# Delta layer of a fused model: the exponentials of the decay in three parts, masks behind the low splits, VectorE's work between the levels of the inverse, and extra multiplications of constants around the turning of x

## What is computed

```python
proj = x @ w_in                                    # 1024 -> 4096 + 16
qkv = silu(causal_depthwise_conv(proj[:, :3072], conv_w))
q = l2_normalize(qkv[:, :1024]) * 128 ** -0.5; k = l2_normalize(...); v = ...
g = -exp(a_log) * softplus(a + dt_bias);  beta = sigmoid(bt)
gc = cumsum(g);  decay = exp(where(causal, gc_i - gc_j, -inf))
a_strict = where(i > j, (k * beta) @ k.T * decay, 0)
u = triangular_solve(a_strict + eye, v * beta)
w = triangular_solve(a_strict + eye, k * beta * exp(gc))
qk = (q @ k.T) * decay
# then, from chunk to chunk: v_new = u - w @ state; o = (q * exp(gc)) @ state + qk @ v_new
y = (rms_norm(o, norm_w) * silu(z)) @ w_o
```

## Time and profile before

| | before |
|---|---|
| median of 3 executions | 2284.34 us |
| their lowest and highest | 2279.2, 2288.88 us |
| the profiled execution | 2281.05 us |
| its span, first to last instruction | 2279.3 us |
| mean granted TensorE clock | 0.986 |
| PE / DVE / ACT / POOL busy | 2181.7 / 1649.5 / 1202.6 / 149.0 us |

### The profile page before, as it was taken

One profiled execution on the slowest core, in us unless ns is written; L12 is line 12 of the kernel. 1 busy time (PEld: TensorE's weight loads), 2 busy tenths in 40 slices (PEclk: granted clock), 3 DMA queues, 4 the chain that ended last, 5 costly groups with the idle time before them and its releaser, 6 DMA issues.

```text
span 2279.3 us, 40684 instructions
## 1 busy us (share of the span) xinstructions
PE 2181.7 (96%) x16637; PEld 2032.2 (89%) x16637; DVE 1649.5 (72%) x2278; ACT 1202.6 (53%) x1717; POOL 149.0 (7%) x175
## 2 busy tenths in 40 slices
PE   7879999999889999999999999999999999999998
PEld 7878978879678887999988899999999988899998
DVE  6674588854858887777865757777877776758776
ACT  5755567763747776433456545333533456545433
POOL 2022000000000000000410001000000220001000
PEclk9999999999999999999999999999999999999999
DMA  8420379959135995555643345555555563346552
GB/s 220 159 93 21 115 272 336 342 181 208 38 96 227 332 328 205 167 172 183 173 144 100 105 137 178 178 181 181 173 174 166 161 179 98 121 152 204 167 200 77
DMA packets 257021, 395.53 MB, mean 174 GB/s; under 512 B 16937, under 2 KB 204194, under 8 KB 256866
## 3 DMA queue, kind: packets, MB, share of 16 engines
q1 hardware_dynamic: 251874, 380.15, 49.8%
q0 software_dynamic: 4880, 13.13, 3.2%
q10 hardware_dynamic: 112, 0.05, 0.0%
HBM read 385.43 MB, written 7.86 MB: 173 GB/s over the span
## 4 chain that ended last, share of the span: by engine, by line
PE 49%; DVE 5%; ACT 3%; DMA 2%; issue 1%; ACTq 0%; DVEq 0%; SPq 0%
PE psum_banks L345 15%; PE psum_banks L347 14%; PE psum_banks L346 14%; DVE weights_low L754 2%; DMA weight_ring<-w_in 2%; PE psum_banks L3300 1%; ACT weights_high L1960 1%; PE psum_banks L3306 1%; PE psum_banks L3325 1%; ACT weights_high L748 1%; DVE source_low L617 1%; PE psum_banks L3335 0%; PE psum_banks L3366 0%; DVE rstd L637 0%; DVE h L780 0%
## 5 line engine op out<-in xcount | busy, mean ns | idle before, releaser
L345 PE MATMUL psum_banks<-source_high,weights_high 128*128 128x272 f32 (+1 forms) x2656 | 780.5, 294 | 21.0 <-DVE weights_low L1967 9.2
L347 PE MATMUL psum_banks<-source_high,weights_low 128*128 128x272 f32 (+1 forms) x2656 | 765.3, 288 | 0.0
L346 PE MATMUL psum_banks<-source_low,weights_high 128*128 128x272 f32 (+1 forms) x2656 | 764.5, 288 | 0.0
L345 PEld LDWEIGHTS psum_banks<-source_high,weights_high 128*128 128x128 f32 x2656 | 508.2, 191 | 29.0 <-DVE weights_low L1967 10.8
L346 PEld LDWEIGHTS psum_banks<-source_low,weights_high 128*128 128x128 f32 x2656 | 508.6, 192 | 1.0
L347 PEld LDWEIGHTS psum_banks<-source_high,weights_low 128*128 128x128 f32 x2656 | 507.5, 191 | 0.0
L1967 DVE TENSOR_TENSOR weights_low<-weight_ring,weights_high 128x2048 fp32r<-128x2048 f32 x102 | 236.2, 2315 | 181.8 <-ACT weights_high L1960 181.3
L748 ACT ACTIVATE weights_high<-weight_ring 128x2048 fp32r<-128x2048 f32 x131 | 242.4, 1910 | 182.7 <-PE psum_banks L347 181.5
L754 DVE TENSOR_TENSOR weights_low<-weight_ring,weights_high 128x2048 fp32r<-128x2048 f32 x131 | 293.1, 2289 | 62.4 <-ACT weights_high L748 62.2
L1960 ACT ACTIVATE weights_high<-weight_ring 128x2048 fp32r<-128x2048 f32 x102 | 194.6, 1908 | 63.2 <-PE psum_banks L347 46.3
L345 PE MATMUL psum_banks<-hidden_high,weights_high 128*128 128x272 f32 (+1 forms) x704 | 203.5, 289 | 1.1 <-DVE h L780 1.0
(11 more groups left out here) (516 smaller groups left out, 3834.2 us busy)
## 6 DMA issues: line engine op xcount, KB each, us to landing
weight_ring<-ffn_w_in SPq DMA_DIRECT2D x88, 1024.0 KB, 6.7
weight_ring<-w_in SPq DMA_DIRECT2D x48, 1024.0 KB, 5.2
weight_ring<-ffn_w_out SPq DMA_DIRECT2D x44, 1024.0 KB, 4.9
weight_ring<-moe_w_down SPq DMA_DIRECT2D x24, 1024.0 KB, 6.8
weight_ring<-moe_w_gate SPq DMA_DIRECT2D x44, 512.0 KB, 4.9
weight_ring<-moe_w_up SPq DMA_DIRECT2D x44, 512.0 KB, 6.5
weight_ring<-gdn_w_in SPq DMA_DIRECT2D x16, 1024.0 KB, 6.4
more_ring<-moe_w_gate SPq DMA_DIRECT2D x32, 512.0 KB, 4.9
```

The source lines that it names most:

```text
L345: pe.matmul(out, w_hi, x_hi, start=start, stop=False)
L346: pe.matmul(out, w_hi, x_lo, start=False, stop=False)
L347: return pe.matmul(out, w_lo, x_hi, start=False, stop=stop)
```

## The change

1. **PE, start.** Ten multiplications of `full_ones` by itself (128x128, f32) stand ahead of `turn_x`, fourteen between it and tile 0. Nobody reads them. The wait for the constant moves ahead of them.
2. **PE, square sums.** Behind tile 12 none, then 7; 8 and 9; 10 and 11; 12; none behind 17; from 18 on as before.
3. **ScalarE.** `decay` is in three parts at t = 9, 10, 11: first the exponentials of the row and the two small ones, which wait for `rows` only; then that of QK, which waits for both masks; then that of A. `silu(7)` to `silu(12)` move to t = 12, 13, 14, two at each.
4. **VectorE, masks.** From t = 5 and 6 to t = 6 and 8, so that each stands behind a `lin.low` and a `conv`.
5. **VectorE, inverse.** q times the decays moves behind level 0, `lin.low` of panel 16 behind level 1, `fall` behind level 3.

```diff
--- before.py
+++ after.py
@@ -2196,8 +2196,13 @@
                         mm = turn(3 + 2 * t, lambda h: v[:, h, chunk[t]])
                     mm.then_inc(pe_n.sem, 1)
 
+                summed_behind = {12: [], 13: [7], 14: [8, 9], 15: [10, 11], 16: [12], 17: []}
+                pe.wait_ge(pr.ones_set.sem, pr.ones_set.at(2))
+                for _ in range(10):
+                    pe.matmul(ps[:, 2, 0:P], pr.full_ones, pr.full_ones, start=True, stop=True)
                 turn_x()
-                pe.wait_ge(pr.ones_set.sem, pr.ones_set.at(2))
+                for _ in range(14):
+                    pe.matmul(ps[:, 2, 0:P], pr.full_ones, pr.full_ones, start=True, stop=True)
                 for t in range(GDN_OUT):
                     lin.multiply(pe, t, source.hi, source.lo, arrive if t == 0 else None)
                     if t == 0:
@@ -2206,8 +2211,9 @@
                         turn_params()
                     if t == 3:
                         decay_rows()
-                    if 0 <= t - 5 < GDN_V:
-                        square_sum(t - 5)
+                    for n in summed_behind.get(t, [t - 5]):
+                        if 0 <= n < GDN_V:
+                            square_sum(n)
                     if t >= GDN_OUT - 6:
                         prepare(t - (GDN_OUT - 6))
                 for n in range(6, 9):
@@ -2321,13 +2327,17 @@
                     do(act.activation(soft, neg_abs, ACT.Exp))
                     act.activation(soft, soft, ACT.Ln, bias=1.0).then_inc(act_n.sem, 1)
 
-                def decay():
-                    act.wait_ge(dve_n.sem, dve_n.at(D_MASK))
-                    act.activation(flat4(QK), flat4(QK), ACT.Exp)
-                    act.activation(flat4(A), flat4(A), ACT.Exp)
-                    act.activation(flat(exp_row[:, :, :]), flat(bank2(6)), ACT.Exp)
-                    act.activation(exp_gc, gc, ACT.Exp)
-                    act.activation(to_last, to_last, ACT.Exp).then_inc(act_n.sem, 1)
+                def decay(part):
+                    if part == 0:
+                        act.wait_ge(dve_n.sem, dve_n.at(D_ROWS))
+                        act.activation(flat(exp_row[:, :, :]), flat(bank2(6)), ACT.Exp)
+                        act.activation(exp_gc, gc, ACT.Exp)
+                        act.activation(to_last, to_last, ACT.Exp)
+                    elif part == 1:
+                        act.wait_ge(dve_n.sem, dve_n.at(D_MASK))
+                        act.activation(flat4(QK), flat4(QK), ACT.Exp)
+                    else:
+                        act.activation(flat4(A), flat4(A), ACT.Exp).then_inc(act_n.sem, 1)
 
                 def sums_out(p):
                     act.wait_ge(ss_mm.sem, ss_mm.at(2 * p + 2))
@@ -2367,9 +2377,12 @@
                         act.wait_ge(pe_n.sem, pe_n.at(P_AB))
                         act.activation(ab[:, :, :], ps[:, 3, 0:32].rearrange("p (t c) -> p t c", t=2), ACT.Copy).then_inc(act_n.sem, 1)
                         small()
-                    if t == 9:
-                        decay()
-                    if 2 <= t < 22:
+                    if t in (9, 10, 11):
+                        decay(t - 9)
+                    elif t in (12, 13, 14):
+                        silu(2 * t - 17)
+                        silu(2 * t - 16)
+                    elif 2 <= t < 22:
                         silu(t - 2)
                     if t >= 7 and t % 2 and t <= 21:
                         sums_out((t - 7) // 2)
@@ -2547,8 +2560,8 @@
                         steps()
                     if t == 4:
                         rows()
-                    if t in (5, 6):
-                        masked(t - 5)
+                    if t in (6, 8):
+                        masked(t // 2 - 3)
                     if t in (24, 25):
                         unit(t - 24)
                     if t in (27, 29):
@@ -2557,9 +2570,6 @@
                     first(t)
                 dve.wait_ge(pe_n.sem, pe_n.at(P_V[1]))
                 dve.tensor_tensor(V[:, 1], bank2(5), heads(beta[:, 1, :]), mul).then_inc(dve_n.sem, 1)
-                lin.low(dve, lin.next_panel(GDN_OUT - 2))
-                dve.tensor_tensor(q[:, :, chunk[1]], q[:, :, chunk[1]], exp_row[:, :, :], mul)
-                do(dve.tensor_tensor(fall, exp_gc, beta, mul))
 
                 def left(ap, s, b):
                     return ap[s, :, s].rearrange("p h (m b) -> p h m b", b=2 * b)[:, :, :, 0:b]
@@ -2581,6 +2591,12 @@
                         else:
                             x = XT[:, t, :, P // 2:P]
                             inv[t].end(dve.tensor_tensor(x, x, bank2(4 * t)[:, :, P // 2:P], sub))
+                    if lev == 0:
+                        dve.tensor_tensor(q[:, :, chunk[1]], q[:, :, chunk[1]], exp_row[:, :, :], mul)
+                    if lev == 1:
+                        lin.low(dve, lin.next_panel(GDN_OUT - 2))
+                    if lev == 3:
+                        do(dve.tensor_tensor(fall, exp_gc, beta, mul))
                 lin.low(dve, 17)
 
                 for p in range(2):
```

## The result

| | before | changed |
|---|---|---|
| median | 2284.67 us (4 runs) | 2267.01 us (4 runs) |
| lowest and highest | 2279.2, 2288.88 | 2265.99, 2269.02 |
| profiled execution, and its span | 2281.05, 2279.3 | 2266.14, 2264.3 |

What follows compares the result with a forecast made beforehand. PE was taken as the bound, with gains only where it waits or runs slowly in the delta layer; 5.7 + 7.1 + 1.8 = 14.6 us gave 2266.4 or 2269.7, stated as 2268 us, range 2260 to 2279.

Steps and rivals of the forecast that it cites:

- the forecast's own signs: Expected in the profile: named waits at tiles 11 to 13, first subtraction 3.7 us after the values, q under 2.6 us.
- Exponentials: Tiles 9 to 17: splitting them cuts PE's waits, 2.3 of 8.1 us left, gain 5.7 us.
- the eight tiles without waits: From tile 9's eviction to tile 17's: eight tiles need 26.4 us, against 34.46 before.
- 1.7 us to spare: Panel 6 lands at 61.6, ScalarE asks at 63.3; a start faster by more than that loses the surplus.
- Inverse: Level 1 starts at 164.3 instead of 169.72, level 2 at 170.8 instead of 177.86: gain 7.1 us.
- by a hair: Levels 1 and 2: moved q and split just fit VectorE's 3.12 us idle gaps; otherwise 4.7 us joins the chain.
- Rival 2: Inverse: GpSimd in the way, q and split come onto the chain, 2.4 instead of 7.1; 2273 us, chance 0.12.
- Constants: Start: tile 0's records at 0.12 us bring 2.0, later start costs 0.3; gain about 1.8 us.
- down again: Narrow `decay_gates` behind tile 0: clock falls there as before, so tile 1's 1.5 us is not counted.
- Rival 1: Start: clock comes late, tile 0 up to 3.4 us later, gain 11.8, 2271 us; chance 0.17.
- Masks: Moving VectorE's two masks: gain 0, since no PE wait had them as the late ones.
- Nothing behind the layer: After the delta layer: nothing should eat the gain, since panel loads wait for free slots and move with the compute.

Runs made afterwards that it cites:

- e5b: Changed kernel without the 24 multiplications of constants at the start; median 2269.24 us, ratio 0.9943.
- e3: Kernel before with only VectorE's three operations moved between the levels of the inverse; median 2275.30 us, ratio 0.9964.
- e8b: Changed kernel with only the fourteen multiplications behind the turns of x, without the ten ahead; median 2267.49 us, ratio 0.9933.
- e10: Changed kernel with the 16 narrow multiplications of the decay gates woven into tile 1; median 2270.94 us, ratio 0.9951.
- e6: Changed kernel with q's multiplication and `fall` behind level 3, the low split of panel 16 behind level 4; median 2267.51 us, ratio 0.9932.
- e1: Kernel before with only the 24 multiplications of constants at the start; median 2282.66 us, ratio 0.9994.
- e9: Changed kernel with GpSimd's fill, load and store of the rpb table held back until VectorE's convolution of tile 12; median 2271.00 us, ratio 0.9944.
- e11: Changed kernel with the rpb store held back, q behind level 3 and the split behind level 4; median 2271.88 us, ratio 0.9955.
- e12: The changed kernel measured again unaltered, beside its variants; median 2268.68 us, ratio 0.9938.
- e7b: Changed kernel with only the ten multiplications ahead of the turning of x, without the fourteen; median 2270.42 us, ratio 0.9945.
- e2: Kernel before with only the exponentials in three parts and the square sums moved; median 2279.12 us, ratio 0.9978.
- e4: Kernel before with only the two masks moved behind the low splits; median 2283.81 us, ratio 1.0002.

## Why the prediction was right

**The sum.** 14.6 was forecast, 2268 us; the medians give 17.7 and 2267.01, and the profiles 14.9, of which 13.1 at the layer's mark and 1.9 in the rest, which no edit touches. Of the 13.1, 3.0 are there at tile 9, 4.8 from 9 to 17, 0.4 from there to the values and 4.9 in the inverse. So each of the three mechanisms acted where it was placed, but that the total came within 1 us is in part luck: two parts were too large, by 0.5 (exponentials, with the 0.4) and 2.2 (inverse), one too small by 1.2, and the rest of the program varies by 9 us between profiles. Several of the forecast's own signs failed: the wait at tile 12 is 1.47 us (under 1 was expected), that behind tile 13 is 0.82 (1 to 2), the first subtraction comes 4.9 us after the values' end (3.7), and q takes 3.31 (under 2.6).

**Exponentials: right, a little too large.** 5.7 forecast, 4.8 measured between the marks. The waits left were 2.3 in the sum and 2.29 in the profile, though not in the places forecast (0.7 and 1.6 there, 1.47 and 0.82 here). The step that was off is the eight tiles without waits, 26.4 in the sum and 27.4 in the changed kernel and in e5b. By the new order a ninth square sum, about 0.4 us, falls between the two marks; it is missing behind tile 17, which is the 0.4 gained from there to the values. The other 0.6 was not traced. The forecast had 1.7 us to spare on panel 6's landing and said that a faster start would use it up: the start was 3.0 faster at tile 9, and ScalarE waited 0.67. Without the constants (e5b) there is no such wait, the one at tile 12 is 0.70 as in the sum, and the part brings 5.6.

**Inverse: the mechanism right, the size by the run.** 7.1 forecast; e3, e8b and e10 gave 7.0, the changed kernel 4.9. Of the 2.1 missing, e6 shows 0.6 to be GpSimd's turns, the fit "by a hair", which held in the profiles at the upper clock only; the other 1.5 is a low clock in level 0, which the sum left out. Of the 7.1, 1.6 was itself a low clock: before, level 1 took 8.14 us, since its records ran at the low clock behind the wait of 5.19 us. So in the changed kernel the low clock moved from level 1 to level 0. Rival 2 happened in small and for the reason named.

**Constants: under-sized, by a clock that the sum did not have.** 1.8 forecast, 3.0 measured at tile 9. By tile 5 the changed kernel leads by 1.5 us, near the forecast, but by other terms: tile 0 starts 0.8 earlier and not 0.3 later, since the turns and so the splits ran faster, and its records bring 2.3; then 1.5 are lost, since gates and tile 1 take longer than before (the clock at 0.50 from 18 us). The other 1.5 come behind tile 5, where PE waits 2.54 us in both kernels. Before, the clock fell after that wait, and in the changed kernel it did not (the same window, before and changed):

```profile
44.00:50.00 6.00, 5.16 (x29) 5.11 (x29) 5.89 (x7) 1.46 (x2) 0.00 (x0) 0.72 1.01 218
...
44.00:50.00 6.00, 6.00 (x51) 5.95 (x51) 5.29 (x7) 1.20 (x3) 0.00 (x0) 1.00 1.02 218
```

The table shows both cases: from tile 5 to tile 9 it takes 17.5 us with the fall (before, e1, e3, e5b, e8b, e9, e11) and 16.0 without (changed, e12, e6b, e7b, e10); e2 and e4 had the late panel there. e1 and e9 reach the same tile 9 by the other way: at tile 5 they are 1.5 us ahead of the changed kernel, and behind it the clock falls. With both sets and the gates in a row tile 9 comes at 56.65 to 56.83 (changed, e1, e6b, e9, e12), and once at 55.19 (e11); without constants at 59.13 to 60.30 (before, e3, e5b). So the constants are worth about 3 us at tile 9, and how much of it comes where differs from run to run. The step that failed is the clock behind tile 0: the sum had it "down again" in the gates "as now" and counted nothing at tile 5. Why it falls after one of these waits and not after the other was not found.

Rival 1 did not happen: with the ten ahead of them the turns ended at the upper clock. The rule of the Trainium skill named there (TensorE: Matmul & The Clock Gate, Part 4), that turns do not count as PE being busy, is not borne out by e2, e3 and e4, which have no constants. PE's first work there is the turns of x, at 6.3 to 6.7 us, and behind them the turn of the convolution's rows takes 0.25 us, as at the upper clock, where it takes 0.37 before. Before, then e3:

```profile
9.80 0.37 PE L2143 MATMUL psum_banks<-consts_common,conv_rows 96*128 96x96 f32 x1
...
9.57 0.25 PE L2143 MATMUL psum_banks<-consts_common,conv_rows 96*128 96x96 f32 x1
...
12.50:15.00 2.50, 2.33 (x11) 2.36 (x12) 1.37 (x3) 1.70 (x4) 0.00 (x0) 0.53 1.09 364
```

The window is e3's: PE had no work for 2.8 us, and the clock fell with the first records of tile 0. In before, e5b and e8b the last turns still ran at the lower clock. So turns alone were followed by the upper clock in three of six profiles, and by tile 0 it was gone again.

**Masks: nothing**, as forecast (1.0002); e4 shows that they can come onto the chain where a panel is late. **Nothing behind the layer ate the gain**, as forecast, as far as can be told beside the 9 us by which the rest varies.

## What to carry to other kernels

Read a small gain at a mark inside the program, right behind what was changed: here 3 us at tile 9 were plain in the profiles, while the untouched rest moved by 9 us between them. Then set two marks and not one: the same 3 us came by two different ways, and one profile of a variant (e10) looked like a gain that a kernel without the edit (e11) had too. When a long stall of one engine is split up, ask at once what else had hidden under it; here it was a panel's landing behind another queue's bulk store. And an instruction moved into another engine's idle gap has the gap's length to itself only if no third engine takes turns with it there.

## What the runs showed of the hardware

- A 1 MB load issued 1.6 to 1.7 us after the first instruction of a 3.5 MB store from GpSimd took 27 us (panel 5 in e4 and e2), one issued 0.2 or 0.8 us after it 5.8 (before) and 6.4 us (e3). Held back to 84 or 85 us, the store left panel 6 at 6.0 us for 24.5, and a later panel came 3.78 and 4.25 us late (e9, e11).
- VectorE's operations with two operands in SBUF and GpSimd's 128x1024 product took turns by whole instructions: the same multiplication took 1.22 us (e6b), 2.31 (e3) and 3.31 (changed), depending only on when it asked. In the changed kernel it ends 1.1 us after one of GpSimd's products, and GpSimd's next, 2.36 us elsewhere, takes 3.36. The Trainium skill (SBUF — State Buffer, Who interferes with whom) describes such an exclusive lock, and these rows agree.
- Behind twenty records of constants (4.64 us) and the turns, tile 0 ran at the upper clock though PE had waited 3.21 us ahead of it (e7b). Behind turns alone the clock was up too in three profiles (e2, e3, e4), and at 0.50 again within 0.3 us of tile 0's start, after 2.8 to 3.0 us without work.
- With the 16 narrow multiplications of the gates in a row, the clock was at 0.50 during tile 1 in eleven profiles (in e1 and e9 for a part of it) and at 1.00 in two (e8b, e11). The one profile with them woven between wide ones (e10) had 1.00, which by itself tells nothing.
- Behind the same wait of 2.5 us at tile 5 the clock fell for 3.4 us in some profiles, which cost 1.5 us, and did not in others.
